# Inverse row sums of an attention spread over the partitions by two DMA transfers instead of four TensorE transposes per block

## What is computed

```python
def _attend(q, k, v):
    s = jnp.einsum('btkgd,bskd->bkgts', q, k).astype(jnp.float32) * (HEAD_DIM ** -0.5)
    p = jax.nn.softmax(s, axis=-1).astype(v.dtype)
    return jnp.einsum('bkgts,bskd->btkgd', p, v)
...
    x = x + gt * ((o_lat * jax.nn.silu(gate[:, n_ctx:])) @ w_out)
```

## Time and profile before

| what | value |
|---|---|
| median of 3 runs | 1211.07 us |
| lowest, highest | 1210.99, 1212.01 us |
| the profiled execution | 1209.13 us |
| its span, first to last instruction | 1207.3 us |
| TensorE busy | 1159.2 us, 96% |
| VectorE busy | 825.5 us, 68% |
| ScalarE busy | 498.4 us, 41% |
| GpSimd busy | 422.1 us, 35% |

### The profile page before, as it was taken

How to read it: one execution, slowest core, us unless ns; L and a number is a source line. 1 busy time by engine, 2 the same in 40 slices (tenths; PEclk the granted TensorE clock), 3 DMA queues, 4 the chain that set the end, 5 groups by cost and what they waited for, 6 DMA issues and landing times.

```text
span 1207.3 us, 16923 instructions
## 1 busy us (share of the span) xinstructions
PE 1159.2 (96%) x6610; PEld 956.2 (79%) x6610; DVE 825.5 (68%) x1264; ACT 498.4 (41%) x924; POOL 422.1 (35%) x330
## 2 busy tenths in 40 slices
PE   3899999999999999999999999999999999999996
PEld 2678879887888987878888888876877777777885
DVE  5699839989925356136839968249888888884237
ACT  3445455220014542134523442246666666664012
POOL 4800000000000002532211112248888888887232
PEclk9899999999999999999999999999999999999998
DMA  9934776425521846203121122330000000000403
GB/s 340 363 114 133 181 221 243 140 91 207 175 88 53 294 176 231 70 36 124 51 70 36 36 79 79 88 122 9 10 18 10 18 18 10 19 9 27 156 26 132
DMA packets 81023, 129.83 MB, mean 108 GB/s; under 512 B 12944, under 2 KB 43024, under 8 KB 80144
## 3 DMA queue, kind: packets, MB, share of 16 engines
q1 hardware_dynamic: 71120, 113.96, 28.2%
q10 hardware_dynamic: 9824, 14.80, 3.5%
HBM read 97.81 MB, written 30.93 MB: 107 GB/s over the span
## 4 chain that ended last, share of the span: by engine, by line
PE 82%; DVE 13%; DMA 2%; ACT 2%; issue 1%; POOL 1%; ACTq 0%; DVEq 0%
PE ps L1860 9%; PE ps L1862 9%; PE ps L1861 9%; PE ps L1871 5%; PE ps L1872 5%; PE ps L1873 5%; DVE region_d L1113 3%; PE ps L2144 3%; PE ps L2174 3%; PE ps L2173 3%; PE ps L2172 3%; PE ps L2222 2%; PE ps L2224 2%; PE ps L2223 2%; PE ps L2193 2%; PE ps L2191 2%
## 5 line engine op out<-in xcount | busy, mean ns | idle before, releaser
L675 POOL TENSOR_TENSOR region_b<-region_b,region_d 128x512 f32<-128x512 f32 x20 | 26.3, 1329 | 472.0 <-DVE region_d L1513 472.0
L1860 PE MATMUL ps<-w_hi,a_hi 128*128 128x512 f32 x448 | 177.7, 397 | 5.6 <-DVE b_lo L1201 4.3
L1861 PE MATMUL ps<-w_lo,a_hi 128*128 128x512 f32 x448 | 175.4, 392 | 0.0
L1862 PE MATMUL ps<-w_hi,c_lo 128*128 128x512 f32 x368 | 143.3, 389 | 0.0
L1871 PE MATMUL ps<-a_hi,w_hi 128*128 128x512 f32 (+1 forms) x384 | 138.0, 359 | 0.0
L1872 PE MATMUL ps<-b_lo,w_hi 128*128 128x512 f32 (+1 forms) x384 | 136.0, 354 | 0.0
L1873 PE MATMUL ps<-a_hi,w_lo 128*128 128x512 f32 (+1 forms) x384 | 136.0, 354 | 0.0
L668 POOL TENSOR_TENSOR w_lo<-weight_ring,w_hi 128x2048 fp32r<-128x2048 f32 x14 | 65.1, 4650 | 185.5 <-ACT w_hi L724 185.5
L1607 DVE TENSOR_REDUCE small<-ps 128x1 f32<-128x1280 f32 x64 | 95.0, 1484 | 40.2 <-PE ps L2144 40.2
L697 POOL TENSOR_TENSOR region_c<-region_c 128x512 f32<-128x512 f32 x80 | 110.0, 1375 | 28.1 <-ACT region_c L1084 25.4
L1860 PEld LDWEIGHTS ps<-w_hi,a_hi 128*128 128x128 f32 x448 | 84.8, 189 | 25.3 <-issue 6.3
(11 more groups left out here) (250 smaller groups left out, 2671.5 us busy)
## 6 DMA issues: line engine op xcount, KB each, us to landing
weight_ring<-in_w_mod SPq DMA_DIRECT2D x10, 2048.0 KB, 9.1
weight_ring<-in_we_in SPq DMA_DIRECT2D x10, 1024.0 KB, 5.6
weight_ring<-in_wo_in SPq DMA_DIRECT2D x10, 1024.0 KB, 5.2
weight_ring<-cop_t_scratch SPq DMA_DIRECT2D x4, 1536.0 KB, 8.4
region_c<-in_w_mod SPq DMA_DIRECT2D x2, 2048.0 KB, 20.9
bop_scratch<-region_d ACTq DMA_DIRECT2D x16, 256.0 KB, 2.9
cop_t_scratch<-region_d SPq DMA_DIRECT2D x8, 512.0 KB, 7.8
weight_ring<-bop_scratch SPq DMA_DIRECT2D x2, 2048.0 KB, 9.8
```

What stands on the lines that cost most here:

```text
L1860: te.matmul(o, th, wh[:, k % 4], start=k == 0, stop=False)
L1861: te.matmul(o, th, wl[:, k % 4], start=False, stop=False)
L1862: last = te.matmul(o, tl, wh[:, k % 4], start=False, stop=k == KT - 1)
```

## The change

The four transposes of `over_sums` go. In their place SyncE stores the 128 x 4 inverse sums to DRAM (16 bytes from each partition) and, once they have landed, loads all 512 numbers into every partition of a free SBUF stretch, `over`. There they lie in the order (query, head), so the gate product reads them with a stride of four words. The gate product and the output move from tile 7 to tile 9 on VectorE, behind the negated maxima; ScalarE's rounding of the output moves from tile 9 to tile 1 of the next block, and GpSimd's rest of the output from tile 0 to tile 3. The query transposes wait for the reciprocal instead of the gate product. Two semaphores of the first layer are merged into one (`y_hi` into `mix_hi`), and the counts that wait on them follow.

```diff
+        rinv_d = nc.dram_tensor("rinv_scratch", (2, P, HPK), F32, kind="Internal").ap()
...
+        over = RC[:, 4608:5120]
...
+            def spread_inverse(i):
+                sp.wait_ge(s_a_ri, i + 1)
+                sp.dma_start(rinv_d[i % 2], rinv).then_inc(s_ri_out, 16)
+                sp.wait_ge(s_ri_out, 16 * (i + 1))
+                if i:
+                    sp.wait_ge(s_a_gr, i)
+                sp.dma_start(over, rinv_d[i % 2].rearrange("(o q) h -> o (q h)", o=1).broadcast_to([P, 512])).then_inc(s_ri_in, 16)
+
             for i in range(2 * LT):
                 if i >= 2:
                     sp.wait_ge(s_a_gr, i - 1)
                 sp.dma_start(gbuf[:, i % 2], gate_d[i // 2, i % 2].rearrange("p h q -> p (h q)")).then_inc(s_gate_in[i % 2], 16)
+                if i:
+                    spread_inverse(i - 1)
+            spread_inverse(2 * LT - 1)
...
-                if t == 0 and i >= 2:
+                if t == 3 and i >= 2:
                     output_rest(i - 2)
...
-                if t == 9 and i:
-                    output_round(i - 1)
+                if t == 1 and i >= 2:
+                    output_round(i - 2)
...
+            output_round(2 * LT - 2)
             output_round(2 * LT - 1)
...
-                dve.wait_ge(s_a_rt, i + 1)
-                v.tensor_tensor(GR, gbuf[:, i % 2], ps[:, 7, :], ALU.mult).then_inc(s_a_gr, 1)
+                dve.wait_ge(s_ri_in, 16 * (i + 1))
+                v.tensor_tensor(GR.rearrange("p (h q) -> p h q", q=P), gbuf[:, i % 2].rearrange("p (h q) -> p h q", q=P),
+                                over.rearrange("p (q h) -> p h q", h=HPK), ALU.mult).then_inc(s_a_gr, 1)
 
             def sums_inverse(i):
                 dve.wait_ge(s_a_sm, i + 1)
+                if i:
+                    dve.wait_ge(s_ri_out, 16 * i)
                 v.reciprocal(rinv, ps[:, 7, 0:HPK]).then_inc(s_a_ri, 1)
...
-                if i and t == 7:
+                if i + 1 < 2 * LT and t == 8:
+                    neg_max(i + 1)
+                if i and t == 9:
                     gate_over_sums(i - 1)
                     output(i - 1)
-                if i + 1 < 2 * LT and t == 8:
-                    neg_max(i + 1)
...
                 if i >= 3:
-                    pe.wait_ge(s_a_gr, i - 2)
+                    pe.wait_ge(s_a_ri, i - 2)
...
-            def over_sums(i):
-
-                pe.wait_ge(s_a_ri, i + 1)
-                for h in range(HPK):
-                    last = tr(ps[:, 7, P * h:P * h + P], rinv[:, h:h + 1].broadcast_to([P, P]))
-                last.then_inc(s_a_rt, 1)
...
-                if i and t == 6:
-                    over_sums(i - 1)
...
-            over_sums(2 * LT - 1)
```

More of the change, by code:

```diff
@@ L285, in build @@
             sem("a_qT"), sem("a_qh"), sem("a_ql"), sem("a_mx"), sem("a_max"), sem("a_nt"), sem("a_nm"))
-        s_a_ri, s_a_rt, s_w_half = sem("a_ri"), sem("a_rt"), sem("w_half")
+        s_a_ri, s_ri_in, s_w_half = sem("a_ri"), sem("ri_in"), sem("w_half")
         s_v_hi, s_v_lo, s_a_ph, s_a_pld, s_a_plp = (
@@ L296, in build @@
             sem("u_in"), sem("u_in3"), sem("gb_in"), sem("y_in"), sem("y_in3"), sem("k_dd"), sem("ga_half"), sem("pchain"), sem("exp"), sem("v_nm"))
-        s_y_hi, s_y_in2 = sem("y_hi"), sem("y_in2")
+        s_y_in2 = sem("y_in2")
+        s_ri_out = sem("ri_out")
         ld_x = [sem(f"ld_x{i}") for i in range(5)]
@@ L921, in y_round @@
                 act.wait_ge(*((s_y_in, 32) if fb < 2 else ((s_y_in2, s_y_in3)[fb - 2], 16)))
-                copy(yh[:, fb], yT[:, fb]).then_inc(s_y_hi, 1)
+                copy(yh[:, fb], yT[:, fb]).then_inc(s_mix_hi, 1)
             for j in range(16):
@@ L940, in _ @@
                     y_round(1)
-            a.activation(small[:, 335:336], epsc, ACT.Sigmoid).then_inc(s_y_hi, 1)
+            a.activation(small[:, 335:336], epsc, ACT.Sigmoid).then_inc(s_mix_hi, 1)
             weights_round(("glu", 0))
@@ L1454, in mix_rest @@
             def mix_rest(fb):
-                dve.wait_ge(s_mix_hi, FB + fb + 1)
+                dve.wait_ge(s_mix_hi, 2 * FB + fb + 2)
                 v.tensor_tensor(B_lo[:, fb], GB[:, fb], hi[:, fb].bitcast(F32), ALU.subtract).then_inc(s_mix_lod, 1)
@@ L1466, in _ @@
                     weights_rest(("glu", 0))
-                dve.wait_ge(s_y_hi, fb + 1 + (fb >= 2))
+                dve.wait_ge(s_mix_hi, FB + fb + 1 + (fb >= 2))
                 v.tensor_tensor(yl[:, fb], yT[:, fb], yh[:, fb].bitcast(F32), ALU.subtract).then_inc(s_mix_lod, 1)
```

## The result

The changed kernel takes 1222.52 us (median of 5 runs, 1220.39 to 1224.16), the kernel before 1211.07 in the same comparison: ratio 1.0095, 95% interval 1.008 to 1.011. It is slower by 11.45 us, outside the range of the prediction and on the other side. Its profiled execution took 1222.33 us around a span of 1220.5, which is 13.2 us longer than the span of 1207.3 before.

A forecast was written before the change was run, and what follows sets the result against it. TensorE was taken to bound the kernel: 7.0 us gained from the transposes, less 4.9 for stalls of 0.38 in 13 blocks behind GpSimd, net 2.1, so 1209.0 us against 1211.07; range 1203.5 to 1216.0.

The forecast's parts named there:

- The bound before, and the gain: Attention: TensorE is the bound, and removing 16 sets of transposes at 0.44 us each gains 7.0 us.
- The strided product: VectorE's gate product, reading one operand four words apart, takes 1.2 us; 0.67 if the stride is free.
- The transfers: Store 2.6, load 3.2, issues and wait 0.3: 6.1 us between reciprocal and gate product, hidden by the 7.4 us covered.
- fourth rival: Transfers late: beyond 7.4 us each microsecond is a stall in full; 9 us would give 1230 us; chance 6%.
- GpSimd's round: GpSimd's work in one attention block becomes 18.75 us, longer than TensorE's 18.37, and so decides the block.
- The turn at tile 7: VectorE's subtraction of tile 7 gets its turn against GpSimd at once; a miss would cost 1.1 us more.
- Every stall delays half of the next one away: GpSimd restarts on tile 1's exponential, before TensorE's stall at the row maximum, so only half the debt counts per block.
- third rival: Strided product and missed turn together delay the first head's row maximum: 0.79 us a block, 1214.3 us; chance 20%.
- at nothing: Edits forecast to cost no time, among them ScalarE's rounding of the output at tile 1 of the next block.
- fit: ScalarE's rounding copy, 0.63 us, has room between the output's end at 904.4 and tile 1's exponential at 905.58.
- GpSimd's rest of the output at tile 3: Its 1.25 us fill no new time in GpSimd's work; its tile 6 subtraction comes 0.8 later, about 2 us free.
- The tail: After the last block the gate product waits 6 us for the transfers, with nothing on the path.

The follow-up runs named there:

- e1: The changed kernel with the gate product's second operand read contiguously from PSUM, transfers kept, division by the row sums left out: 1204.90 us.
- e4: The kernel before without the transposes, the gate product at tile 7 reading PSUM, division by the row sums left out: 1206.79 us.
- e7: The changed kernel with inverse sums stored head by head in 4-byte pieces, so that load and gate product are contiguous: 1311.63 us.
- e6: The changed kernel with only GpSimd's rest of the output moved from tile 3 to tile 5: 1212.79 us.
- e3: The changed kernel with ScalarE's rounding of the output moved from tile 1 to 3 and GpSimd's rest from tile 3 to 5: 1213.34 us.
- e11: The changed kernel with four useless 128x4 fills on GpSimd ahead of its subtraction of tile 6: 1212.04 us.
- e13: The changed kernel with only ScalarE's rounding of the output moved from tile 1 to tile 2: 1214.74 us.
- e9: The changed kernel with one useless 128x16 fill on GpSimd ahead of its subtraction of tile 6: 1218.03 us.
- e2: The changed kernel with the gate product reading the loaded sums contiguously, so in the wrong order: 1205.37 us.

## Why the prediction was wrong

**The bound before, and the gain.** Right. TensorE set the end, and the transposes were on its path; what their removal gives depends on who stands behind: 0.38 a block in e1, 0.29 in e4, against 0.44. "The negated maxima now come ahead of gate and output, which helps" fits the difference between those two; no run moves them alone.

**The strided product.** Right in kind, and a little too dear: 1.07 us against the 1.2 taken, 0.67 to 0.69 in the contiguous form. The Trainium skill (SBUF — State Buffer, Door 1) wants two hits in a 16-byte line for the full rate and yet allows a stride of four fp32; the measurement decides for the first.

**The transfers.** Right in the sum, with luck: the store was taken 1.2 us too long (1.4 against 2.6) and the load 1.0 too short (4.2 against 3.2). Together with the second issue they are some 5.9 us against 6.1, all covered (no gate product waits for a load in the blocks). e7 shows the edge of that cover, and that the fourth rival lacked a term: behind a stall of more than 5 us TensorE's clock costs some 2 to 3 us more in each block, by estimate.

**GpSimd's round.** Right within 0.15: 18.75 forecast, 18.90 in e6, where GpSimd is the bound. With the turn caught the change is then a kernel of 1212 to 1213 us (e3, e6, e11), where the forecast was 1209.0. Of those 4 us, 13 x 0.15 = 2 are this round, and 15 x 0.06 = 0.9 the transposes, which gave 0.38 at best; the rest isn't resolved.

**The turn at tile 7: the first step that failed.** The forecast let VectorE have "its first turn at once". The prediction saw that it was "caught or missed by 0.1 us" and gave the caught turn the larger part, 62% in all. It is missed, by 0.10 us (923.60 against 923.50), in 13 blocks on end. The Trainium skill (SBUF — State Buffer, SBUF: two separate sides) says that whichever of the two engines starts first holds the shared ports for its whole instruction and the other blocks; the trace agrees (1.76 us against 0.95 in e6, for the same subtraction). How close the border is the runs show too: the turn is caught with a request 0.03 us ahead of GpSimd's issue (e11, 862.44 against 862.47) and missed with one 0.01 ahead (e1).

**"Every stall delays half of the next one away": the step that failed in size.** The third rival had stride and missed turn together, with a debt of 0.17 + 0.1 + 1.1 = 1.37, or 1.57 with GpSimd's lag, and halved it. The chain behind the request has the length that the rival gave it: from 903.90 to the end of the row maximum at 912.26 are 8.36 us, against 6.88 + 0.5 + 1.1 = 8.48. The stall measured is 19.69 - 18.37 = 1.32 us a block: the whole debt, and not half of it. The sum of the prediction with that number gives 283.5 - 15 x 0.44 + 13 x 1.32 = 294.1, which is the distance of the row sums that was measured. The reason that was given for the half, that GpSimd restarts on the exponential of tile 1 before the stall, was undone by an edit of this same change that the prediction put **at nothing**: ScalarE's rounding of the output now stands ahead of that exponential, and waits for the output (1.2 us in each of 14 blocks, by the waits). That the copy would "fit" held only with the turn caught, and the fallback, that "TensorE needs it only two tiles later", looked at TensorE and not at GpSimd, which starts its whole round there. e13 moves the rounding alone and has a stall of 0.85 where that rival had 0.79, and 1214.74 us where it had 1214.3. So it is the rounding's place that hands on the whole debt; that half of it is what is left otherwise is shown by e13 alone, and there in another rhythm.

**GpSimd's rest of the output at tile 3, also at nothing.** Its work was free, but where it stands sets the phase of GpSimd's instructions against VectorE's request at tile 7; at tile 5 the turn is caught (e6).

**The tail.** Right: a wait of 6.73 us for the transfers, nothing on the path.

So the slower result was the third rival's mechanism, at a chance of 20%, with a stall that was 0.53 us a block, 7 us in all, too small. What stays open: the 3.0 us by which the unchanged stage ahead of the attention differs between the two profiled executions is taken for scatter, because the experiments scatter there by more. That the turn is caught or missed block after block is shown by e9, e11, e6 and e2; what made GpSimd late for once in e9 is not known; why e13 settles in a third rhythm between the two was not tried further.

## What to carry to other kernels

Where two engines take turns, a cost is not a sum: write down who asks when, and if a request and its rival's issue lie within some tenths of a microsecond, price both cases and give neither the better odds. Before a stall is taken to fade, follow the waiting instruction to everything queued behind it on its engine, and look for the engine that starts its round on one of those; if there is one, the stall can be handed on whole, as here. And a cheap test of such a phase is to delay the winner on purpose: 0.2 us of useless work brought back 10 us here.

## What was not expected of the hardware

A stride of 16 bytes in one fp32 operand in SBUF costs VectorE 1.07 instead of 0.69 us for 128x512, and ScalarE 1.15 instead of 0.63. A 2 KB store costs 1.4 us in 128 pieces of 16 bytes and 8.4 us in 512 pieces of 4 bytes; the load that gives all partitions the same 2 KB took 3.9 to 4.2 us after the first and 4.8 after the second. And two engines that take turns can settle in either of two rhythms in the same program: 19.72 or 18.9 us a block in e9, with a request only 0.05 us late in the slower one. The slower one went on for six blocks, until one late instruction of GpSimd ended it; the faster one then lasted to the end of the stage. In e7 idle times of TensorE of 5.0 to 5.7 us were followed by a granted clock of 0.50 to 0.72 over the next 6 us.
